# Four loops over the rounds of a recurrent mixer, written out round by round

## What is computed

```python
mod = silu(c) @ w_ada[l] + b_ada[l]        # 2048 x 12288 weights per layer
```

```python
def step(S, inp):
    r_t, w_t, k_t, v_t, kk_t, a_t = inp
    sa = einsum('bhij,bhj->bhi', S, -kk_t)
    S = S * w_t[:, :, None, :] + sa[..., None] * (kk_t * a_t)[:, :, None, :] \
        + v_t[..., None] * k_t[:, :, None, :]
    return S, einsum('bhij,bhj->bhi', S, r_t)
```

## Time and profile before

| | us |
|---|---|
| time, median of 3 runs | 3154.0 (3150.7 to 3159.11) |
| time of the profiled execution | 3154.8 |
| its span, first to last instruction | 3153.0 |

### The profile page before, as it was taken

The page is one execution under the profiler, slowest core; times in us unless marked ns, Lnnn a source line. Parts: engine busy times, 40 slices in busy tenths (PEclk is TensorE's granted clock), DMA queues, the critical chain, the costliest instruction groups (busy, mean ns, idle before and its releaser), DMA issues.

```text
span 3153.0 us, 48841 instructions
## 1 busy us (share of the span) xinstructions
PE 2871.3 (91%) x17315; PEld 2176.1 (69%) x17315; DVE 1646.6 (52%) x2172; ACT 1094.0 (35%) x1377; POOL 165.9 (5%) x209
## 2 busy tenths in 40 slices
PE   6899788889899999999878997888898999999997
PEld 1578555567688888888615785555677888888885
DVE  0466545444655555555515655555356555555554
ACT  0244322224344444444203443222234444444442
POOL 1000111110000000000010001111000000000000
PEclk9999988889899999999989998888898999999998
DMA  9765666645366666666496655666454666666662
GB/s 363 240 181 157 199 205 215 215 149 186 114 187 187 190 188 187 189 190 186 140 319 218 176 162 177 216 216 216 162 160 137 187 190 187 188 190 187 186 190 90
DMA packets 317241, 600.57 MB, mean 190 GB/s; under 512 B 23184, under 2 KB 29288, under 8 KB 316584
## 3 DMA queue, kind: packets, MB, share of 16 engines
q1 hardware_dynamic: 309488, 592.90, 59.3%
q10 hardware_dynamic: 7608, 5.60, 0.6%
HBM read 595.28 MB, written 3.15 MB: 190 GB/s over the span
## 4 chain that ended last, share of the span: by engine, by line
PE 76%; issue 10%; DVE 6%; DMA 5%; ACT 1%; POOL 1%; DVEq 1%; SPq 0%; ACTq 0%; POOLq 0%
PE bank L758 74%; DMA rawW<-in_w_ada 5%; PE bank L1110 1%; DVE xs L1291 1%; DVE AE L1495 0%; DVE ksq L1469 0%; DVEq L286 0%; SPq L335 0%; DVE BF L1495 0%; DVE tf L1272 0%; POOL qst L667 0%; DVE cs L1453 0%; DMA out_new_v<-proj 0%; PE bank L1042 0%; DVE x L1293 0%
## 5 line engine op out<-in xcount | busy, mean ns | idle before, releaser
L1219 DVE TENSOR_TENSOR loW<-rawW,hiW 128x1024 fp32r<-128x1024 f32 x592 | 724.9, 1226 | 737.0 <-ACT hiW L376 736.6
L376 ACT ACTIVATE hiW<-rawW 128x1024 fp32r<-128x1024 f32 x592 | 627.1, 1061 | 962.6 <-PE bank L758 960.6
L758 PE MATMUL bank<-hiW,actH 128*128 128x512 f32 (+1 forms) x2304 | 901.0, 391 | 18.3 <-DVE loW L1219 15.8
L758 PE MATMUL bank<-loW,actH 128*128 128x512 f32 (+1 forms) x2304 | 893.8, 388 | 0.0
L758 PE MATMUL bank<-hiW,actL 128*128 128x512 f32 (+1 forms) x2304 | 893.6, 388 | 0.0
L758 PEld LDWEIGHTS bank<-hiW,actH 128*128 128x128 f32 x2304 | 435.9, 189 | 109.0 <-DVE loW L1219 16.0
L758 PEld LDWEIGHTS bank<-hiW,actL 128*128 128x128 f32 x2304 | 435.3, 189 | 89.1
L758 PEld LDWEIGHTS bank<-loW,actH 128*128 128x128 f32 x2304 | 435.8, 189 | 87.8 <-issue 1.0
L758 PE MATMUL bank<-rawW,csR 128*32 128x512 f32 x1536 | 321.6, 684 | 107.5 <-DMA rawW<-in_w_ada 51.5
L758 PE MATMUL bank<-hiW,ffH 128*128 128x512 f32 x704 | 281.5, 400 | 3.2 <-DVE ffL L1589 3.2
L758 PE MATMUL bank<-hiW,ffL 128*128 128x512 f32 x704 | 280.9, 399 | 0.0
(11 more groups left out here) (246 smaller groups left out, 2264.4 us busy)
## 6 DMA issues: line engine op xcount, KB each, us to landing
rawW<-in_w_ada SPq DMA_DIRECT2D x384, 512.0 KB, 7.9
rawW<-in_w_gate SPq DMA_DIRECT2D x176, 512.0 KB, 3.7
rawW<-in_w_up SPq DMA_DIRECT2D x176, 512.0 KB, 3.7
rawW<-in_w_down SPq DMA_DIRECT2D x176, 512.0 KB, 3.6
rawW<-in_w_in SPq DMA_DIRECT2D x144, 512.0 KB, 3.6
rawW<-in_w_out SPq DMA_DIRECT2D x64, 512.0 KB, 3.6
rawW<-in_w_in SPq DMA_DIRECT2D x16, 160.0 KB, 2.3
x<-in_x_prompt SPq DMA_DIRECT2D x1, 1024.0 KB, 8.3
```

What stands on the lines that cost most here:

```text
L376: act.activation(hiW[:, c % LEAD, :, 0:width], rawW[:, c % SLOTS, :, 0:width], ACT.Copy).then_inc(hi_ready, 1)
L758: return pe.matmul(out, a, b, start=start, stop=stop, skip_group_check=True)
L1219: TT(loW[:, slot, :, 0:width], rawW[:, slot, :, 0:width], hiW[:, c % LEAD, :, 0:width].bitcast(F32), ALU.subtract).then_inc(lo_ready, 1)
```

## The change

The loop over the rounds becomes a loop of the program that writes the kernel, so that each engine's instruction stream holds the four rounds one behind another, and `f` is a constant in each. The number of the layer stays a register, and so `it` and `qa` (the count of weight tiles) are still computed at run time. The inner loops of ACT and POOL stay, once in each round. The work, its order on each engine, the waits and the transfers are the same.

```diff
@@ ACT: rwkv(l)
-                with act.Fori(0, FT) as f:
+                for f in range(FT):
                     it = act.snap(l * FT + f)
                     qa = act.snap(l * Q_LAYER + Q_ADA2 + f * 8)
                     act.activation(wS[:], wla[:, :, bass.ds(f * P, P)], ACT.Copy)
...
@@ POOL: rwkv(l)
-                with pool.Fori(0, FT) as f:
+                for f in range(FT):
                     it = pool.snap(l * FT + f)
...
@@ PE: rwkv(l)
-                with pe.Fori(0, FT) as f:
+                for f in range(FT):
                     it = pe.snap(l * FT + f)
                     qa = pe.snap(l * Q_LAYER + Q_ADA2 + f * 8)
...
@@ DVE: rwkv(l)
-                with dve.Fori(0, FT) as f:
+                for f in range(FT):
                     it = dve.snap(l * FT + f)
                     qa = dve.snap(l * Q_LAYER + Q_ADA2 + f * 8)
```

## The result

The changed kernel takes 3110.45 us (median of four, 3105.81 to 3113.75) against 3153.52 us in the same session: 0.986 of the time before, with a 95% interval of 0.9842 to 0.9879.

The account below looks back on a forecast made before the run. The recurrent mixer was taken to be bound by a chain of small results between engines, with PE stalled at loop edges. 18.8 + 2.6 + 3.7 + 0 = 25.1 us off 3154.8 gave 3130 us, range 3118 to 3145.

Parts of the forecast that it names:

- part 4: TensorE's clock in the A-matrix stage: longer idle before it can only lower it; taken 0, bounds 0 to 11 us loss.
- part 2: ACT table loads: those at L502 go, worth nothing; the sigmoid's at L508 goes in two first rounds, 2.6 us gained.
- Part 3: Register arithmetic for addresses, mainly on DVE, goes as the round number becomes constant: 3.7 us gained, bounds 0 and 9.
- Part 1: PE's six loop-edge stalls go, saving DVE's waits before scan and row copies: 18.8 us, bounds 0 and 25.6.
- Weights: Rival: modulation matmuls would wait for weight transfers instead of code, so part 1 gives nothing: 3148.5 us, chance 0.05.
- The other cause: Rival: PE's edge stall is no code fetch and stays in straight code: 3148.5 us, chance 0.04.
- Streaming: Rival: written-out code must be fetched on DVE, ACT and GpSimd, exposing misses: 3180 to 3206 us, chance 0.06.
- The larger gain: Rival: DVE's order is freed more, up to all of PE's idle comes back: 37 us, 3118 us, chance 0.07.

Follow-up runs that it names:

- 1: Only PE's loop over the rounds written out, ACT, DVE and POOL keep theirs, against the kernel before: 3129.95 us, 0.9934.
- 3: PE and DVE written out, ACT and POOL keep their loops, against the kernel before: 3124.66 us, 0.9914.
- 7: Changed kernel plus six idle matmuls before PE's wait for KR: 3109.13 us, 0.9862 of the kernel before.
- 8: Kernel before, with its loops, plus six idle matmuls before PE's wait for KR: 3132.08 us, 0.9943.
- 6: Changed kernel, but PE waits for DVE's old round to end before the first modulation tile: 3150.7 us, 0.9991 of the kernel before.
- 5: PE loops over pairs of rounds, ACT, DVE and POOL written out, against the kernel before: 3122.18 us, 0.9906.
- 11: Changed kernel with idle matmuls in four of PE's waits per round: 3084.48 us, 0.9782 of the kernel before.

## Why the prediction was wrong

**The step that failed is part 4.** "A longer idle before it can only lower the clock there", taken as 0 with a loss of 11 as its bound: the stage gained 8.5 us. Two things were wrong in it. The idle did not grow: 3.18 us before, 3.02 after in round 2, and in the two first rounds it fell from 2.96 and 3.10 to 1.55 and 1.68. And the stage as it stood was not at the upper level: the earlier trace rows looked at its second half alone (0.87), where the clock was already recovering; over all of it the clock was 0.72. There was something to win that the text didn't look for. What changed in the later rounds is what PE does ahead: in the old round the stalled first tile ran straight into the second, whose chunks had yet to arrive; now there is a pause between them, the slots fill, and the second runs dense, and the low stretch of the clock lies there. That this decides is argued and not shown: the tile is dense in experiments 1 and 3 too, and three and all six of their later stages are long. In the two first rounds (3.4 of the 8.5 us) PE's wait for KR got shorter, through the table load of part 2. The loss that part 4 feared does occur in experiment 3, where the idle grew to 3.9 to 5.0 us and the gain was 0.2.

Why 3.0 to 3.2 us of idle leave the clock up in four rounds of the changed kernel and take it down in two (3.0 and 3.1) stays open. In these two it falls 1 us before the stage begins. Filling the wait removes the loss in every round of either kernel (7, 8).

**Part 3 was mis-sized**, 8.4 for 3.7, inside its bounds of 0 to 9. I read only gaps in front of instructions, and left out that an instruction itself gets shorter (L1444) and that ACT's last copy, for which DVE waits, comes earlier too. The wait for it is 3.9 us now; before it was:

```profile
DVE actL L1562 <- ACT actH L565: 6.0, 8, 0.7
```

**Part 1 was right**: its 18.8 us stood for the waits in front of the scan and of the row copies, which gave 18.7 and 2.0. That DVE's order comes next, and not PE's whole idle, is what experiments 1 and 6 show. **Part 2 was right** in the two loads (2.7 for 2.6), apart from the 3.4 us that they are worth one stage later; it was wrong about those at L502 (3). The sum thus fell short by 19.2 us: 8.5 in part 4, 4.7 in part 3, 1.9 in part 1, 0.1 in part 2 and 4.0 in stretches that it left out.

**The rivals.** Weights didn't take the place of the stall. The other cause, one that straight code keeps, is out: the stall left with the branch (1, 5). Streaming cost nothing that the trace shows: nine more packets on q14 where 12 to 18 were expected, and DVE's only wait called "issue" of that size is still the one at the layer's edge (L1638, 3.7 us). The larger gain came nearer in size, for the wrong reason: its 37 us were to come from PE's idle, of which the chain could not use more. That the stall is a fetch of code is not measured by itself; for it speak q8's packets, which go with the taken branch in number and in time (5).

On this the Trainium skill (Runtime: NRT & Kernel Launch, Instruction fetch mechanics) says that a taken branch to code that is no longer loaded stalls until it is fetched, while straight code is streamed with its cost mostly hidden. The trace agrees: 5.3 us at an edge, none between straight rounds.

## What to carry to other kernels

Look at the loop-head branch of every engine: where one takes microseconds and the others tens of nanoseconds, write out that loop, and then the others too, since most of what they save only counts once the first is gone. Before calling a stage's clock harmless, take its whole window at the granted clock; where the same matmuls run slow, fill the wait ahead of them with matmuls that nobody reads, few enough to end before the wait does. Loads and copies that lie in the shadow of a stall have a price as soon as the stall goes.

## What was not expected of the hardware

- Idle matmuls pay: 6 + 4 + 1 + 2 in a round made the kernel before 40 us faster and the changed one 26 us, though each adds work to the engine that is busy 91% of the span.
- A taken edge on PE cost 6.1 us at the longest when its loop body held two rounds, 5.85 us with one.
- q8, the queue taken for that of PE's code, moved 108 packets with six taken edges on PE, 100 with two and 96 with none (98 in 11, with its added matmuls).
- One DVE instruction of 128 x 256 (L1444) took 562 ns with a column address from a register and 353 ns with a fixed one; two others like it took the same with either. The gap in front of all three was longer with the register.
